# One GpSimd instruction per tap for both channel tiles of a prompt convolution, with the tap broadcast along the tokens

## The chip, the cores and the metric

The kernel runs on one core of a Trainium2 chip. The metric is device time in microseconds for one execution of the whole program, the median of the runs of one kernel. Instruction durations come from one profiled execution.

## The reference, cut to what matters

Two layers of a hybrid decoder trunk are computed for a prompt of 256 tokens and for 8 sample sequences of 4 tokens. Each layer is a feed-forward half step, a mixer, cross attention and another feed-forward half step. The mixer projects the normalised input once (`w_in`), and three groups use the columns: a gated depthwise convolution, a dilated attention, and an RWKV-7 recurrence. The convolution is this:

```python
glu = cols_a[..., :CONV_CH] * sigmoid(cols_a[..., CONV_CH:])
u = concatenate([hist, glu], axis=1)             # hist: 30 rows, zero for the prompt
y = conv_general_dilated(u, conv_w[:, None, :], window_strides=(1,), padding='VALID',
                         feature_group_count=CONV_CH) + conv_b
# then a layer norm over the 256 channels and silu
```

It has 256 channels and 31 taps, and it multiplies each channel by its own 31 weights.

## The kernel before

Activations lie with channels on the 128 partitions and the tokens along the row: 256 prompt tokens and then 32 sample tokens (T = 288, TP = 256). The 256 convolution channels are two channel tiles.

**Weights.** SP streams the weights in slabs. ScalarE (ACT) rounds each unit of 128x1024 to `w_hi` (line 1336), VectorE (DVE) computes the remainder `w_lo` = raw - `w_hi` (line 1837), and TensorE (PE) multiplies in three passes, hi*hi, lo*hi and hi*lo (lines 641 to 643). There are three such buffers (NW = 3), so that DVE can be at most three units ahead of PE. The order of work on each engine is written out by hand, and every engine is in order.

**The projection stage.** While PE computes the tiles of `w_in`, DVE does, between one `w_lo` and the next, the token shift of the tile that has arrived (`shifted`, lines 1932 and 1934), and pieces of the recurrence's preparation: the decay scan (1981), centring (1990), key norms (1995, 1997, 2002, 2006), products (2011 to 2030), and the 32 sample tokens' convolution (`conv_samples`, 1970 to 1975). Then the recurrence's chunk inverses follow (`block_products` on PE, line 827, with masks and sums on DVE, lines 2075 to 2113).

**The prompt convolution** runs on GpSimd (POOL) alone. `up` holds the 30 rows of history and 256 tokens of both channel tiles, `ycv` is the sum, and `prod` has two buffers of products, so that the products of tap k+1 are made before tap k is summed. For tap 0 the product and the bias go straight to `ycv`. For each other tap there are two `tensor_scalar` instructions (line 513), one for each channel tile, each with the 128 weights of that tap as a pointer to one value in each partition, and one `tensor_tensor` add over both tiles (line 529). POOL waits on its own semaphore before it overwrites `prod` and before it sums. It begins when the last gated tile is there (line 1949). Behind it on POOL's queue are the load of the cross-attention memory and the stores of the layer (lines 532 and 476). The sum of the last tap is waited for by ACT, before it overwrites the place of `prod`, and by PE, for the mean over channels (line 1052).

Of the kernel before, what the change touches and what calls it, by code (L numbers as in the profile page):

```python
# [9 lines left out]
ALU = mybir.AluOpType  # L10
# [3 lines left out]
P = 128  # L14
DEPTH, D_MODEL, D_FF = 2, 1024, 2816
TP, DEC_BATCH, DEC_SEQ = 256, 8, 4
# [7 lines left out]
TAPS = 31  # L24
# [80 lines left out]
PAR, NPAR = {}, 0  # L105
# [124 lines left out]
def program(nc, x_in, mem_in, stream, small, consts, conv_hist, wkv_in, copies, outs, known=None):  # L230
    (y_out, conv_out, kv_out, shift_out, wkv_p_out, wkv_s_out, memk_out, memv_out) = outs
    known = known or {}
    with ExitStack() as ctx:
# [45 lines left out]
        def take(*dims):  # L279
            n = int(np.prod(dims))  # L280
            v = arena[:, top[0]:top[0] + n]
            top[0] += n
            assert top[0] <= ARENA, top[0]
            if len(dims) == 1:
                return v
            names = "abcd"[:len(dims)]
            return v.rearrange(f"p ({' '.join(names)}) -> p {' '.join(names)}",
                               **{k: d for k, d in zip(names[1:], dims[1:])})
# [45 lines left out]
        up = take(2, HIST + TP)  # L334
# [34 lines left out]
        ycv, prod = take(2, T), take(2, 2, T)  # L369
# [50 lines left out]
        def bt(ap):  # L420
# [13 lines left out]
        TL, VL, SL, PL = (Line(s, known.get(n)) for s, n in ((tensor_done, "t"), (vector_done, "v"), (scalar_done, "s"),  # L434
                                                             (pool_done, "p")))
# [6 lines left out]
        @block.sync  # L442
        def _(sp):
            sp.dma_start(x[:], x_in).then_inc(start_landed, 16)

            first = CON["turn"]
            sp.dma_start(con[:, 0:first], consts[:, 0:first]).then_inc(start_landed, 16)
            gains = PAR["conv_w"]
            sp.dma_start(par_all[:, :, 0:gains], small[:, :, 0:gains]).then_inc(par_landed, 16)
            flat = stream.rearrange("l n p c -> (l n) p c")  # L450
            for l in range(DEPTH):
                for n in range(NSLAB):

                    held = n - NSLOT if n >= NSLOT else n + NSLOT * (ROUNDS - (n >= REST))
                    line, name = (VL, ("lo", UNIT_OF_SLAB[held] + 1)) if held in UNIT_OF_SLAB else (TL, ("slab", held))
                    if held == 0:
                        sp.wait_ge(vector_done, VL.value(l - 1, ("next", "lo", 1)))
                    else:
                        sp.wait_ge(line.sem, line.value(l, name) if n >= NSLOT else line.value_before(l, name))
                    sp.dma_start(slots[:, n % NSLOT, :], stream[l, n]).then_inc(slab_landed[n % NSLOT], 16)  # L460
                    if l == 0 and n == NSLOT + 4:
                        sp.dma_start(con[:, first:], consts[:, first:]).then_inc(con_landed, 16)
                        sp.dma_start(par_all[:, :, gains:], small[:, :, gains:]).then_inc(con_landed, 16)

                    if n % 5 == 4 and n // 5 < len(copies):
                        src, dst = copies[n // 5]
                        sp.dma_start(dst[l], src[l]).then_inc(copied, 16)
            sp.wait_ge(copied, 16 * 6 * DEPTH)


        @block.gpsimd
        def _(pool):
            n_stores = [0]

            def store(dst, src, name):
                pool.dma_start(dst, src).then_inc(stored, 16)
                n_stores[0] += 1
                stores[name] = n_stores[0]

            def presum(l, tag, n):  # L480

                for k in range(1, n):
                    pool.wait_ge(scalar_done, SL.value(l, (tag, "sq", k)))
                    if k > 1:
                        pool.wait_ge(pool_done, PL.value(l, (tag, "added", k - 1)))
                    PL.done(nc.gpsimd.tensor_tensor(sq[:, 0, :], sq[:, 0, :], sq[:, k, :], ALU.add), (tag, "added", k))  # L486

            pool.sem_inc(pool_done, PL.tail)
            PL.begin_prologue()
            presum(-1, "next", EARLY)  # L490
            pool.wait_ge(con_landed, 32)
            for l in range(DEPTH):
                n_stores[0] = 0
                PL.begin_layer()

                presum(l, "mix", EARLY)

                pool.wait_ge(vector_done, VL.value(l, ("ffn1", "x", KT - 1)))
                pool.wait_ge(tensor_done, TL.value(l, ("ffn1", "down", 1)))
                pool.dma_start(us4[:, :, :, 0:HIST], conv_hist[l]).then_inc(layer_landed, 16)  # L500


                pool.wait_ge(vector_done, VL.value(l, ("glu", 1)))
                pool.wait_ge(tensor_done, TL.value(l, ("in", "cols", RAW - 1)))
                par = par_all[:, l, :]

                def products(tap):
                    for ch in range(2):
                        w = par[:, PAR["conv_w"] + ch * TAPS + tap:PAR["conv_w"] + ch * TAPS + tap + 1]
                        bias = par[:, PAR["conv_b"] + ch:PAR["conv_b"] + ch + 1]  # L510
                        out = (prod[:, tap % 2, ch, :] if tap else ycv[:, ch, :])[:, 0:TP]
                        if tap:
                            p_ = nc.gpsimd.tensor_scalar(out, up[:, ch, tap:tap + TP], w, None, ALU.mult)  # L513
                        else:
                            p_ = nc.gpsimd.tensor_scalar(out, up[:, ch, tap:tap + TP], w, bias, ALU.mult, ALU.add)
                        PL.done(p_)
                    PL.done(p_, ("products", tap))

                products(0)
                products(1)  # L520
                for tap in range(1, TAPS):
                    if tap + 1 < TAPS:
                        if tap > 1:
                            pool.wait_ge(pool_done, PL.value(l, ("summed", tap - 1)))
                        products(tap + 1)
                    pool.wait_ge(pool_done, PL.value(l, ("products", tap)))
                    if tap > 1:
                        pool.wait_ge(pool_done, PL.value(l, ("summed", tap - 1)))
                    PL.done(nc.gpsimd.tensor_tensor(ycv[:, :, 0:TP], ycv[:, :, 0:TP], prod[:, tap % 2, :, 0:TP], ALU.add), ("summed", tap))  # L529

                pool.wait_ge(scalar_done, SL.value(l, ("u", 1)))
                pool.dma_start(memx, mem_in).then_inc(mem_landed, 16)
                store(conv_out[l, :, :, 0:HIST], up[:, :, TP:TP + HIST], "conv_p")
                store(conv_out[l, :, :, HIST:].rearrange("p a (b t) -> p a b t", b=DEC_BATCH)[:, 0],
                      us4[:, 0, :, DEC_SEQ:], "conv_s0")
                store(conv_out[l, :, :, HIST:].rearrange("p a (b t) -> p a b t", b=DEC_BATCH)[:, 1],
                      us4[:, 1, :, DEC_SEQ:], "conv_s1")
                pool.wait_ge(vector_done, VL.value(l, "shift_out"))
                store(shift_out[l], shift_o, "shift")

                pool.wait_ge(vector_done, VL.value(l, "roped"))
                pool.wait_ge(scalar_done, SL.value(l, ("in", IN_TILES - 1)))
                store(kv_out[l], qkv[:, G:3 * G, :], "kv")
                pool.wait_ge(vector_done, VL.value(l, ("state", 1)))
                store(wkv_p_out[l], st, "wkv_p")
                pool.wait_ge(vector_done, VL.value(l, "wkv_s"))
                store(wkv_s_out[l], wkv_s, "wkv_s")
                presum(l, "xattn", PRESUM["xattn"])
                pool.wait_ge(scalar_done, SL.value(l, ("kx", KT - 1)))
                store(memk_out[l], kx, "memk")  # L550
                pool.wait_ge(scalar_done, SL.value(l, ("vx", 7)))
                store(memv_out[l], vx, "memv")
                presum(l, "ffn2", PRESUM["ffn2"])
                PL.begin_tail()
                presum(l, "next", EARLY)
            assert n_stores[0] == NSTORE
            pool.wait_ge(vector_done, VL.value(DEPTH - 1, ("final", "h", KT - 1)))
            pool.dma_start(y_out, h[:]).then_inc(stored, 16)
            pool.wait_ge(stored, 16 * (NSTORE * DEPTH + 1))
# [1963 lines left out]
```

## Time and profile before

| what | value |
|---|---|
| median of 3 runs | 1712.31 us (1711.0 to 1713.2) |
| the profiled execution's own time | 1711.11 us |
| its span, first to last instruction | 1709.3 us |
| mean granted TensorE clock | 0.974 |
| busy shares of the span: PE, DVE, ACT, POOL | 94%, 63%, 44%, 17% |
| POOL's products (line 513), 120 instructions | 145.4 us |
| POOL's sums (line 529), 60 instructions | 87.7 us |

The shares are averages over all stages. The convolution runs twice, once in each layer, from 258.9 us to 379.3 us and from 1096.9 us to 1218.1 us of the span.

### The profile page before, as it was taken

How to read it: one execution, taken by the hardware profiler on the slowest of the kernel's cores; microseconds unless marked ns; L12 is line 12 of the kernel's file. 1: busy time of each engine (PE TensorE's matmuls, PEld its weight loads, DVE VectorE, ACT ScalarE, POOL GpSimd, SP SyncE). 2: the span in 40 equal slices, each digit the busy share in tenths (PEclk: the TensorE clock that was granted, in tenths of full speed). 3: DMA queues.
4: the chain of work that ended last, by engine and by line, in shares of the span. 5: the costliest groups of instructions: out<-in, count | busy, mean ns of one | idle time of the engine just before them, and what ended most of it. 6: DMA issues, size and time to landing. Idle time of an engine off the chain costs nothing.

```text
span 1709.3 us, 32132 instructions
## 1 busy us (share of the span) xinstructions
PE 1602.4 (94%) x13704; PEld 1512.7 (88%) x13704; DVE 1071.7 (63%) x1613; ACT 752.4 (44%) x1292; POOL 288.7 (17%) x250
## 2 busy tenths in 40 slices
PE   6999999899899889999999999998988997999996
PEld 6999998786789769999999999888768885999996
DVE  5776469867563357775577754896575642677744
ACT  5444357325453335443454434662254442544433
POOL 0000009990010010000000000399501000100000
PEclk9999999998999989999999999999889998999998
DMA  6666744204545764455355676431234468444450
GB/s 242 254 243 250 294 139 148 94 23 92 211 137 209 285 256 164 160 172 173 147 185 210 222 288 235 147 124 46 59 124 168 170 227 349 168 170 162 160 172 28
DMA packets 39247, 303.72 MB, mean 178 GB/s; under 512 B 4737, under 2 KB 4897, under 8 KB 6305
## 3 DMA queue, kind: packets, MB, share of 16 engines
q1 hardware_dynamic: 36624, 287.74, 46.5%
q0 software_dynamic: 2192, 12.35, 2.5%
q8 instruction: 109, 1.79, 0.4%
q10 hardware_dynamic: 288, 1.57, 0.3%
q14 instruction: 34, 0.27, 0.0%
HBM read 291.88 MB, written 36.83 MB: 192 GB/s over the span
## 4 chain that ended last, share of the span: by engine, by line
PE 79%; DVE 13%; ACT 4%; DMA 2%; issue 1%; SPq 0%; POOL 0%; DVEq 0%; ACTq 0%
PE bank L641 22%; PE bank L643 21%; PE bank L642 21%; DVE w_lo L1837 3%; PE bank L827 3%; DMA slots<-stream 2%; ACT w_hi L1336 1%; PE bank L1252 1%; PE bank L1288 1%; PE bank L1237 1%; DVE h_mem L1853 1%; PE bank L654 1%; ACT arena L1336 1%; PE bank L791 1%; PE bank L1125 1%
## 5 line engine op out<-in xcount | busy, mean ns | idle before, releaser
L1837 DVE TENSOR_TENSOR w_lo<-slots,w_hi 128x1024 fp32r<-128x1024 f32 x386 | 483.4, 1254 | 351.2 <-ACT w_hi L1336 350.6
L641 PE MATMUL bank<-h_hi,w_hi 128*128 128x288 f32 x1936 | 578.6, 299 | 30.1 <-DVE w_lo L1837 14.2
L642 PE MATMUL bank<-h_lo,w_hi 128*128 128x288 f32 x1936 | 572.4, 296 | 0.0
L643 PE MATMUL bank<-h_hi,w_lo 128*128 128x288 f32 x1936 | 570.4, 295 | 0.0
L1336 ACT CAST w_hi<-slots 128x1024 fp32r<-128x1024 f32 x390 | 406.9, 1045 | 296.9 <-PE bank L643 271.5
L641 PEld LDWEIGHTS bank<-h_hi,w_hi 128*128 128x128 f32 x1936 | 363.9, 188 | 37.9 <-issue 15.0
L643 PEld LDWEIGHTS bank<-h_hi,w_lo 128*128 128x128 f32 x1936 | 365.8, 189 | 0.0
L642 PEld LDWEIGHTS bank<-h_lo,w_hi 128*128 128x128 f32 x1936 | 364.7, 188 | 0.3
L486 POOL TENSOR_TENSOR arena<-arena 128x288 f32<-128x288 f32 x39 | 36.9, 945 | 1043.1 <-ACT arena L1376 618.0
L643 PE MATMUL bank<-hid_hi,w_lo 128*128 128x288 f32 x704 | 207.7, 295 | 0.0
L642 PE MATMUL bank<-hid_lo,w_hi 128*128 128x288 f32 x704 | 207.3, 294 | 0.0
L641 PE MATMUL bank<-hid_hi,w_hi 128*128 128x288 f32 x704 | 207.1, 294 | 0.0
L1336 ACT COPY arena<-bank 128x256 f32<-128x256 f32 (+8 forms) x258 | 86.0, 369 | 258.1 <-PE bank L643 117.1
L513 POOL TENSOR_SCALAR arena<-arena,par_all 128x256 f32<-128x256 f32 x120 | 145.4, 1222 | 5.5
L641 PEld LDWEIGHTS bank<-hid_hi,w_hi 128*128 128x128 f32 x704 | 132.1, 188 | 0.0
L643 PEld LDWEIGHTS bank<-hid_hi,w_lo 128*128 128x128 f32 x704 | 132.1, 188 | 0.0
L642 PEld LDWEIGHTS bank<-hid_lo,w_hi 128*128 128x128 f32 x704 | 132.0, 188 | 0.0
L1405 ACT ACTIVATE arena<-arena 128x288 f32<-128x288 f32 x88 | 39.2, 445 | 196.1 <-DVE arena L1868 196.1
L529 POOL TENSOR_TENSOR arena<-arena 128x512 f32<-128x512 f32 x60 | 87.7, 1461 | 0.3
L1868 DVE TENSOR_TENSOR arena<-bank,rs 128x288 f32<-128x288 f32 x88 | 40.3, 457 | 43.3 <-PE bank L643 43.0
L827 PE MATMUL bank<-arena 64*64 64x64 f32 x1488 | 54.0, 224 | 8.8 <-DVE arena L2098 7.2
L827 PEld LDWEIGHTS bank<-arena 64*64 64x64 f32 x1488 | 51.3, 139 | 11.3 <-DVE arena L2098 7.6
(323 smaller groups left out, 2130.8 us busy)
## 6 DMA issues: line engine op xcount, KB each, us to landing
slots<-stream SPq DMA_DIRECT2D x244, 1024.0 KB, 5.0
out_win3k<-win3k SPq DMA_DIRECT2D x2, 4080.0 KB
out_win3v<-win3v SPq DMA_DIRECT2D x2, 4080.0 KB
out_win2k<-win2k SPq DMA_DIRECT2D x2, 2032.0 KB
out_win2v<-win2v SPq DMA_DIRECT2D x2, 2032.0 KB
con<-consts SPq DMA_DIRECT2D x1, 2340.0 KB, 11.0
arena<-mem_in POOLq DMA_DIRECT2D x2, 1024.0 KB, 5.5
out_memk<-arena POOLq DMA_DIRECT2D x2, 1024.0 KB
```

The lines of the kernel that those rows point to most:

```text
L486: PL.done(nc.gpsimd.tensor_tensor(sq[:, 0, :], sq[:, 0, :], sq[:, k, :], ALU.add), (tag, "added", k))
L513: p_ = nc.gpsimd.tensor_scalar(out, up[:, ch, tap:tap + TP], w, None, ALU.mult)
L529: PL.done(nc.gpsimd.tensor_tensor(ycv[:, :, 0:TP], ycv[:, :, 0:TP], prod[:, tap % 2, :, 0:TP], ALU.add), ("summed", tap))
L641: mm(out, lhs[0], rhs[0], start=start, stop=False)
L642: mm(out, lhs[0], rhs[1], start=False, stop=False)
L643: return mm(out, lhs[1], rhs[0], start=False, stop=stop)
L654: i = mm(bank[7][:, 0:n], ones, squares[:, k, 0:n], start=k == 0, stop=k == KT - 1)
L827: i = mm(bank[b][o_, s_], lhs[r_, s_], rhs[r_, s_], start=True, stop=True)
L1336: return SL.done(nc.scalar.copy(out, in_), name)
L1405: SL.done(fn(th[:, t % 2, :], gs[:, t % 2, :], ACT.Tanh, scale=0.5), (tag, "tanh", t))
L1837: D(tt(out, src, hi.bitcast(F32), ALU.subtract), name)
L1868: D(tt(gs[:, t % 2, :], bank[gb][:, 0:T], rs[:], ALU.mult), (tag, "gated", t))
```

## The change

Tap 0 stays as it was. For taps 1 to 30 the two `tensor_scalar` products of 128x256 become one `tensor_tensor` product of 128x512, whose second input is the pair of weights of the tap, each broadcast along the 256 tokens. The sums, the two product buffers and the waits stay.

```diff
+                weights = par[:, PAR["conv_w"]:PAR["conv_w"] + 2 * TAPS].rearrange("p (c k) -> p c k", c=2)
+
                 def products(tap):
+                    if tap:
+                        w = weights[:, :, tap:tap + 1].to_broadcast([P, 2, TP])
+                        p_ = nc.gpsimd.tensor_tensor(prod[:, tap % 2, :, 0:TP], up[:, :, tap:tap + TP], w, ALU.mult)
+                        PL.done(p_, ("products", tap))
+                        return
                     for ch in range(2):
-                        w = par[:, PAR["conv_w"] + ch * TAPS + tap:PAR["conv_w"] + ch * TAPS + tap + 1]
                         bias = par[:, PAR["conv_b"] + ch:PAR["conv_b"] + ch + 1]
-                        out = (prod[:, tap % 2, ch, :] if tap else ycv[:, ch, :])[:, 0:TP]
-                        if tap:
-                            p_ = nc.gpsimd.tensor_scalar(out, up[:, ch, tap:tap + TP], w, None, ALU.mult)
-                        else:
-                            p_ = nc.gpsimd.tensor_scalar(out, up[:, ch, tap:tap + TP], w, bias, ALU.mult, ALU.add)
-                        PL.done(p_)
-                    PL.done(p_, ("products", tap))
+                        p_ = nc.gpsimd.tensor_scalar(ycv[:, ch, 0:TP], up[:, ch, 0:TP], weights[:, ch, 0:1], bias, ALU.mult, ALU.add)
+                        PL.done(p_, ("products", 0) if ch else None)
```

## Rows read from the trace of the kernel before

**Rows 1.** The page: busy shares, the chain that ended last, engines and lines.

```profile
PE 1602.4 (94%) x13704; PEld 1512.7 (88%) x13704; DVE 1071.7 (63%) x1613; ACT 752.4 (44%) x1292; POOL 288.7 (17%) x250
PE 79%; DVE 13%; ACT 4%; DMA 2%; issue 1%; SPq 0%; POOL 0%; DVEq 0%; ACTq 0%
```

**Rows 2.** Busy time by stretch: start:end, length, then each engine's us (instructions), clock.

```profile
258.00:322.00 64.00, 59.01 (x410) 55.39 (x408) 61.99 (x79) 37.63 (x75) 61.87 (x41) 0.97 0.38 132
322.00:380.00 58.00, 51.95 (x1056) 47.43 (x1056) 35.76 (x65) 18.98 (x39) 55.58 (x52) 1.00 0.11 34
1096.00:1160.00 64.00, 59.99 (x428) 56.79 (x427) 59.90 (x84) 37.56 (x75) 62.04 (x40) 1.00 0.41 138
```

**Rows 3.** Busy time of line 529 alone in the same stretches.

```profile
258.00:322.00 64.00, 19.57 (x12) 0.97 0.38 132
...
1096.00:1160.00 64.00, 19.75 (x12) 1.00 0.41 138
```

**Rows 4.** Instructions by line on POOL, whole span.

```profile
L513 POOL TENSOR_SCALAR arena<-arena,par_all 128x256 f32<-128x256 f32 x120 | 145.4, 1222 | 5.5
L529 POOL TENSOR_TENSOR arena<-arena 128x512 f32<-128x512 f32 x60 | 87.7, 1461 | 0.3
```

**Rows 5.** Lines 513 and 529: min/median/max in ns.

```profile
L513 POOL TENSOR_SCALAR arena<-arena,par_all x120: 917/925/3262, 261.2 to 1214.3; 128x256 f32<-128x256 f32 x120
...
L529 POOL TENSOR_TENSOR arena<-arena x60: 1267/1286/2516, 266.7 to 1216.8; 128x512 f32<-128x512 f32 x60
```

**Rows 6.** POOL and PE in order of time, first convolution's end and its reader.

```profile
376.58 2.72 POOL L529 TENSOR_TENSOR arena<-arena 128x512 f32<-128x512 f32 x2
...
402.82 1.81 PE L1052 MATMUL bank<-arena,con 128*128 128x288 f32 x3
```

**Rows 7.** DVE in order of time, projection stage of the first layer.

```profile
284.32 2.32 DVE L1837 TENSOR_TENSOR w_lo<-slots,w_hi 128x1024 fp32r<-128x1024 f32 x1
...
289.79 1.21 DVE L1837 TENSOR_TENSOR w_lo<-slots,w_hi 128x1024 fp32r<-128x1024 f32 x1
...
311.32 1.21 DVE L1837 TENSOR_TENSOR w_lo<-slots,w_hi 128x1024 fp32r<-128x1024 f32 x1
312.45 2.14 DVE L2015 SCALAR_TENSOR_TENSOR arena<-arena 128x864 f32<-128x864 f32 x1
314.51 1.05 DVE L2016 TENSOR_TENSOR arena<-arena 128x864 f32<-128x864 f32 x1
```

**Rows 8.** POOL in order of time, the same stage.

```profile
284.18 1.38 POOL L529 TENSOR_TENSOR arena<-arena 128x512 f32<-128x512 f32 x1
...
289.92 3.13 POOL L513 TENSOR_SCALAR arena<-arena,par_all 128x256 f32<-128x256 f32 x2
...
311.51 2.17 POOL L529 TENSOR_TENSOR arena<-arena 128x512 f32<-128x512 f32 x1
313.77 2.50 POOL L513 TENSOR_SCALAR arena<-arena,par_all 128x256 f32<-128x256 f32 x1
```

**Rows 9.** DVE by line, 258 to 322 us.

```profile
L1837 DVE TENSOR_TENSOR w_lo<-slots,w_hi 128x1024 fp32r<-128x1024 f32 x16 | 22.0, 1373 | 0.2 <-ACT w_hi L1336 0.2
L1932 DVE SCALAR_TENSOR_TENSOR arena<-arena,par_all 128x256 f32<-128x256 f32 x11 | 7.3, 661 | 1.3 <-ACT arena L1459 1.3
...
L1934 DVE SCALAR_TENSOR_TENSOR arena<-arena,par_all 128x32 f32<-128x32 f32 x11 | 4.7, 426 | 0.0
```

**Rows 10.** The same lines' shortest in the span (min/median/max).

```profile
L1932 DVE SCALAR_TENSOR_TENSOR arena<-arena,par_all x22: 380/526/1350, 260.5 to 1134.0; 128x256 f32<-128x256 f32 x22
...
L1934 DVE SCALAR_TENSOR_TENSOR arena<-arena,par_all x22: 237/377/1287, 260.9 to 1134.3; 128x32 f32<-128x32 f32 x22
```

**Rows 11.** DVE by line, 322 to 380 us, and its shortest in the span.

```profile
L2106 DVE TENSOR_TENSOR arena<-arena,con 128x384 f32<-128x384 f32 x8 | 7.5, 939 | 0.0
...
L2106 DVE TENSOR_TENSOR arena<-arena,con x16: 544/700/1679, 336.9 to 1191.7; 128x384 f32<-128x384 f32 x16
```

**Rows 12.** The chain that ended last, shares by line within 258 to 322 us.

```profile
by line: DVE w_lo L1837 23.5%; PE bank L641 7.1%; PE bank L750 6.8%; PE bank L643 6.7%; PE bank L642 6.6%; DVE arena L1932 4.5%; DVE arena L1970 4.0%; DVE arena L1934 3.5%; DVE arena L2022 3.2%; DVE arena L2015 3.2%; DVE arena L1997 3.0%; D
```

## The prediction

> **What bounds the kernel now.** I read the page first. PE is busy for 94% of the span and the chain that ended last runs 79% through PE, 13% through DVE and 0% through POOL [rows 1]. So POOL's own 233 us of convolution [rows 4] are nowhere a term of the time, and a faster POOL gains nothing by being faster. That has to be checked where POOL ends: the last sum of the first layer ends at 376.58 + 2.72 = 379.3 us, and PE reads the sum from 402.8 us [rows 6], with no wait for POOL. The convolution has 23 us to spare. What the change does to the time must therefore come through something that POOL shares with another engine.
>
> Second I read the busy time by stretch. In the projection stage, 258 to 322 us, DVE is busy 61.99 of 64 us, and PE 59.0; in the second layer it is 59.9 and 60.0 [rows 2]. In this stage the chain goes through DVE's lines more than through PE's: line 1837 alone has 23.5%, with 1932, 1970, 1934, 2022, 2015 and 1997 behind it [rows 12]. DVE waits there for hardly anything (0.2 us for ACT at line 1837, 1.3 us at line 1932 [rows 9]). So any microsecond that DVE loses in this stage is lost to the kernel, once in each layer, but for a small lead. The next stage, 322 to 380 us, has DVE busy for 35.8 of 58 us [rows 2]; there a DVE delay counts only when PE waits for that instruction.
>
> Third I laid DVE's and POOL's instructions side by side in time. The sum of line 529 starts at 284.18 and ends at 285.56. DVE's line 1837 starts at 284.32, takes 2.32 us in place of 1.21, and ends at 286.64 [rows 7, 8]: it lost 1.11 us, which is what was left of the sum. The other way round, the sum that starts at 311.51, during a line 1837 that ends at 312.53, takes 2.17 us, 0.90 more than its shortest of 1.267 [rows 5, 7, 8]. It got through exactly when DVE's instruction ended; the next one, line 2015, had started at 312.45 and took 2.14 where its neighbour of the same size, line 2016, took 1.05 [rows 7]. It waited until the sum was over. So a two-input POOL instruction and a DVE instruction that reads two SBUF tensors exclude each other for nearly their whole length, and at this boundary the waiting POOL instruction went ahead of the next DVE instruction.
>
> The products of line 513 behave otherwise. Two of them start at 289.92, while line 1837 runs from 289.79, and that one takes its 1.21 us as if alone. The product at 313.77 takes 2.50 us, and meanwhile line 2016 runs its 1.05 [rows 7, 8]. The single-input product is delayed by DVE but hardly delays DVE.
>
> The Trainium skill, page "SBUF — State Buffer", section "Who interferes with whom", says that the pair of ports that both engines use is an exclusive lock, and that a DVE instruction with two SBUF inputs and a GpSimd instruction that reads SBUF block each other fully. For the sums the trace agrees, with 1.11 us. For the products it doesn't: by that rule line 1837 at 289.79 should have been held up for part of 0.9 us. Which of the two holds for the products decides the sign of this change, and the rule's result is the first rival below.
>
> **The change part by part.**
>
> Removed: 30 pairs of products a layer, 2 x 0.917 = 1.83 us uncontended. Off the path, since POOL isn't on it: 0. What they cost DVE now is small; I come to it in the sum.
>
> Added: 30 `tensor_tensor` products of 128x512 a layer. The trace has no GpSimd product with a broadcast input. The nearest row is the sum of the same opcode and shape, 1.267 us at the shortest [rows 5]; I take it, because size, type and number of inputs are the same. The ends are one `tensor_scalar`, 0.917 us, and two of them, 1.83 us. The broadcast itself I take as free.
>
> What DVE loses now in the stage: 12 sums lie in it in each layer [rows 3]. At 1.11 us each these are 13.3 us; some met DVE in the middle of an instruction and cost less, and the products add a little: three lines alone lose 16 x (1.373 - 1.21) + 11 x (0.661 - 0.380) + 11 x (0.426 - 0.237) = 2.6 + 3.1 + 2.1 = 7.8 us [rows 9, 10], in 38 of the 79 instructions, so 15 us for all is a fair value. DVE's own work in the stage is then 62 - 15 = 47 us, in 79 instructions, 0.6 us each.
>
> What DVE loses after: POOL now has 60 two-input instructions a layer, with nothing between them in which DVE has the ports to itself (today the two products give it that room). If each takes its turn with one DVE instruction, a turn lasts 1.11 + 0.6 = 1.7 us, and 60 of them 103 us, all of it within the stage, since DVE has 79 instructions there. I let 5 of the 60 pass beside DVE instructions that read PSUM or have one input (a choice), and charge 55 x 1.11 = 61 us. The stage becomes 47 + 61 + 2 = 110 us in place of 64. That is 61 - 15 = 46 us more in each layer, 92 in all.
>
> What hides it: DVE's lead over PE. There are only three buffers, and PE waits 64 - 59 = 5 us already [rows 2]. I take off 3 us a layer (a choice; 0 is the other end). -6.
>
> What comes back: today 18 of the 30 sums fall in the next stage, where line 2106 loses 8 x (0.939 - 0.544) = 3.2 us [rows 11]. POOL will be done by the time DVE gets there. With the neighbouring masks I take 4 us a layer on the path. -8.
>
> POOL's end: 258.9 + 103 plus the two products of tap 0 and the passes is about 370 us of the span, near today's, while its readers move back by some 40. The stores and the memory load behind it on POOL's queue wait for later events of ACT and DVE and move with these. The semaphore increments that go away and those waits cost nothing, because POOL is in no chain. PE idles more in the stage, and its granted clock, 0.97 there [rows 2], may fall; PE needs 59 us and gets 110, so even slower matmuls are covered by DVE, and I charge 0.
>
> Sum: 92 - 6 - 8 = +78 us. Against the profiled execution's 1711.1 us this is 1789; the median, 1712.3, is 1.2 us above it, so 1790.
>
> **Rivals.**
>
> *The rule as the page has it: any POOL instruction holds up DVE.* Then today's products cost DVE as much as the sums, and POOL occupies the ports for 61.9 of 64 us [rows 2]. It still would, and the loss in the stage stays at 15 us; but with 30 instructions fewer POOL is done some 20 us sooner in the next stage, and gives back the 4 us there. Time: 1712 - 8 = 1704. For it: POOL is less busy in total. Against: the 1.21 and 1.05 us of lines 1837 and 2016 beside running products [rows 7, 8]. It decides if a single-input product now costs DVE 0.8 us or more. Chance 0.07. This is the case on the other side of zero. By the Trainium skill (same page and section), it would be the outcome.
>
> *The new product holds DVE as briefly as the old one,* because its second input is only two values a row. Then a tap takes POOL about 3.0 us in the stage, 20 sums fall in it instead of 12, 8 x 1.0 more, less 3 of lead and 3 in the next stage: +2 a layer, 1716. Against: the second input is still read as a tensor. Chance 0.10, half of it within the noise.
>
> *DVE wins every second boundary.* Two DVE instructions pass for each POOL instruction: 47/1.2 = 39 turns x 1.11 = 43 us, so the stage grows by 28, less 3 of lead and 2 in the next stage, +23 a layer: 1758. For it: the short DVE instructions (0.24 us, line 1934 [rows 10]) may slip in between two POOL ones. Chance 0.17.
>
> **How the numbers follow.** The forecast, that they take turns, has 0.63 and its own range is 1760 to 1830: below, a 0.917 us product (30 x 0.35 = 10 us less a layer, 1770) with a few more passes; above, all 60 at 1.25 us, no lead and nothing back, 2 x (75 - 15) = +120, 1832; a 1.83 us product alone gives 30 x 0.56 x 2 = +34, 1824. The third rival widens the range to 1740. The first two stay outside with 0.17, and 0.03 for what I haven't thought of. I take 1740 to 1830. 0.2%, 3.4 us, is about what a measurement of this kernel can tell from no change. Slower: 0.63 + 0.17 + 0.05 + 0.01 = 0.86. Same: 0.05 + 0.01. Faster: 0.07 + 0.01.
>
> **What the changed profile would show.** Products of 128x512 at about 1.27 us shortest and well over 1.5 mean. In the projection stage, DVE's line 1837 at 2.3 us in most places, 1932 near 1.5 and 1934 near 1.3, PE waiting for line 1837, and a stage of about 110 us instead of 64. In the next stage, line 2106 at 0.55. I am wrong if line 1837 stays near 1.3 us, if the new product's shortest is far from 1.27, or if DVE's losses don't show up in PE's waits.

## The result and the profile after

The changed kernel takes 1760.7 us (median of 4 runs, 1759.3 to 1763.1) against 1711.9 us for the kernel before beside it. The ratio is 1.0286, 95% interval 1.0268 to 1.0304: 49 us slower. The forecast was slower, 1790, range 1740 to 1830. So the sign was right, and the size was 78 where 49 was measured. The time is nearer to the third rival's 1758; why that is luck stands below.

Line numbers after the convolution's code are one higher than before. The page of the changed kernel:

```profile
PE 1623.0 (92%) x13704; PEld 1529.1 (87%) x13704; DVE 1125.2 (64%) x1613; ACT 754.1 (43%) x1292; POOL 245.4 (14%) x190
...
PE 76%; DVE 16%; ACT 3%; DMA 2%; issue 1%; SPq 0%; DVEq 0%; POOL 0%; ACTq 0%
...
L530 POOL TENSOR_TENSOR arena<-arena 128x512 f32<-128x512 f32 x60 | 107.0, 1783 | 0.3
L512 POOL TENSOR_TENSOR arena<-arena,par_all 128x512 f32<-128x512 f32 x60 | 83.0, 1385 | 4.4
```

POOL has 43 us less to do than in [rows 1], is still 0% of the chain, and the kernel is slower. The chain's share moved from PE to DVE. Both POOL lines together take 190 us against 233 before [rows 4], yet each sum now takes 1.78 us in the mean where it took 1.46. The busy time by stretch, columns as in [rows 2]:

```profile
258.00:350.00 92.00, 69.08 (x408) 63.99 (x407) 91.51 (x80) 38.20 (x75) 89.19 (x57) 0.85 0.26 91
350.00:380.00 30.00, 26.83 (x695) 25.38 (x696) 21.45 (x44) 9.38 (x19) 7.00 (x6) 1.00 0.20 65
1124.00:1216.00 92.00, 68.55 (x408) 63.66 (x407) 91.55 (x79) 37.90 (x74) 89.69 (x57) 0.85 0.26 90
```

The DVE instructions that filled 62 of 64 us now fill 91.5 of 92, in both layers, while PE waits. DVE by line in the first stretch, which answers to [rows 9]:

```profile
L1838 DVE TENSOR_TENSOR w_lo<-slots,w_hi 128x1024 fp32r<-128x1024 f32 x16 | 23.7, 1482 | 0.0
L1933 DVE SCALAR_TENSOR_TENSOR arena<-arena,par_all 128x256 f32<-128x256 f32 x11 | 12.9, 1170 | 0.0
L1935 DVE SCALAR_TENSOR_TENSOR arena<-arena,par_all 128x32 f32<-128x32 f32 x11 | 10.6, 961 | 0.0
L1971 DVE TENSOR_TENSOR arena<-arena,par_all 128x248 f32<-128x248 f32 x8 | 10.3, 1351 | 0.1
```

The two token-shift lines grew from 0.66 to 1.17 us and from 0.43 to 0.96 us in the mean, and the weight remainder in the first line only from 1.37 to 1.48. Why shows in DVE's and then POOL's instructions in order of time:

```profile
263.22 1.21 DVE L1838 TENSOR_TENSOR w_lo<-slots,w_hi 128x1024 fp32r<-128x1024 f32 x1
264.36 1.51 DVE L1933 SCALAR_TENSOR_TENSOR arena<-arena,par_all 128x256 f32<-128x256 f32 x1
265.80 1.02 DVE L1935 SCALAR_TENSOR_TENSOR arena<-arena,par_all 128x32 f32<-128x32 f32 x1
266.74 1.21 DVE L1838 TENSOR_TENSOR w_lo<-slots,w_hi 128x1024 fp32r<-128x1024 f32 x1
...
341.81 2.28 DVE L1838 TENSOR_TENSOR w_lo<-slots,w_hi 128x1024 fp32r<-128x1024 f32 x1
```

```profile
263.21 2.38 POOL L530 TENSOR_TENSOR arena<-arena 128x512 f32<-128x512 f32 x1
265.67 1.10 POOL L512 TENSOR_TENSOR arena<-arena,par_all 128x512 f32<-128x512 f32 x1
266.74 2.38 POOL L530 TENSOR_TENSOR arena<-arena 128x512 f32<-128x512 f32 x1
```

The sum at 263.21 waits while 1838 runs, then holds up 1933 until 265.6. The product at 265.67 holds up 1935 until about 266.6. 1935 is 32 elements long and over at once; 1838 and the next sum start in the same hundredth, 266.74, and 1838 goes first. So three DVE instructions pass for two of POOL here, not two for two. In the last 22 us of the stage DVE's other instructions are long too (128x864 most of them). There the turns are one for one, and line 1838 takes 2.06 to 2.30 us, as at 341.81; its other twelve take 1.21, or 1.45 once.

### The profile page after: what moved, and what is told of

It is laid out like the page before. It is cut to its first block, busy times and chain, and to the rows that moved or that the text cites. A ratio compares the mean times of both kernels' runs of the same rounds, so it can differ in the third digit from the quotient of the medians.

```text
span 1759.1 us, 32072 instructions
## 1 busy us (share of the span) xinstructions
PE 1623.0 (92%) x13704; PEld 1529.1 (87%) x13704; DVE 1125.2 (64%) x1613; ACT 754.1 (43%) x1292; POOL 245.4 (14%) x190
## 4 chain that ended last, share of the span: by engine, by line
PE 76%; DVE 16%; ACT 3%; DMA 2%; issue 1%; SPq 0%; DVEq 0%; POOL 0%; ACTq 0%
PE bank L642 21%; PE bank L644 21%; PE bank L643 20%; DVE w_lo L1838 4%; PE bank L828 3%; DMA slots<-stream 2%; DVE arena L1933 1%; DVE arena L1971 1%; DVE arena L1935 1%; ACT w_hi L1337 1%; PE bank L1253 1%; PE bank L1289 1%; PE bank L1238 1%; DVE h_mem L1854 1%; PE bank L655 1%
## 5 line engine op out<-in xcount | busy, mean ns | idle before, releaser
L642 PE MATMUL bank<-h_hi,w_hi 128*128 128x288 f32 x1936 | 588.7, 304 | 62.1 <-DVE w_lo L1838 43.8
L643 PE MATMUL bank<-h_lo,w_hi 128*128 128x288 f32 x1936 | 581.4, 300 | 0.0
L644 PE MATMUL bank<-h_hi,w_lo 128*128 128x288 f32 x1936 | 579.0, 299 | 0.0
L642 PEld LDWEIGHTS bank<-h_hi,w_hi 128*128 128x128 f32 x1936 | 372.8, 193 | 73.2 <-DVE w_lo L1838 22.3
L644 PEld LDWEIGHTS bank<-h_hi,w_lo 128*128 128x128 f32 x1936 | 374.3, 193 | 0.0
L643 PEld LDWEIGHTS bank<-h_lo,w_hi 128*128 128x128 f32 x1936 | 373.3, 193 | 0.3
L530 POOL TENSOR_TENSOR arena<-arena 128x512 f32<-128x512 f32 x60 | 107.0, 1783 | 0.3
L512 POOL TENSOR_TENSOR arena<-arena,par_all 128x512 f32<-128x512 f32 x60 | 83.0, 1385 | 4.4
L1869 DVE TENSOR_TENSOR arena<-bank,rs 128x288 f32<-128x288 f32 x88 | 40.2, 457 | 43.3 <-PE bank L644 43.1
```

The costliest lines, as they stand in the source:

```text
L512: p_ = nc.gpsimd.tensor_tensor(prod[:, tap % 2, :, 0:TP], up[:, :, tap:tap + TP], w, ALU.mult)
L642: mm(out, lhs[0], rhs[0], start=start, stop=False)
L643: mm(out, lhs[0], rhs[1], start=False, stop=False)
L644: return mm(out, lhs[1], rhs[0], start=False, stop=stop)
L1869: D(tt(gs[:, t % 2, :], bank[gb][:, 0:T], rs[:], ALU.mult), (tag, "gated", t))
```

## The experiments

Each comparison is with the kernel before on the same chip.

**Products alone and sums alone.** One kernel drops the sums, the other the products of taps 1 to 30.

```diff
# products alone (the loop's body, cut)
-                    PL.done(nc.gpsimd.tensor_tensor(ycv..., ycv..., prod[:, tap % 2, :, 0:TP], ALU.add), ("summed", tap))
+                    pool.wait_ge(pool_done, PL.value(l, ("products", tap - 1)))
+                    products(tap)
# sums alone (the same loop, cut)
-                        products(tap + 1)
...
+                    PL.done(nc.gpsimd.tensor_tensor(ycv..., ycv..., up[:, :, tap:tap + TP], ALU.add), ("summed", tap))
```

> The changed kernel without the 60 sums of line 530 (the convolution's result is then only tap 0 and the last products lie unused). My theory: each two-input GpSimd instruction costs VectorE about 0.8 us in the projection stage, product or sum alike; 30 products a layer cost 24 us where the kernel before lost 15, and the next stage is free of GpSimd (4 to 6 us back a layer), so 1712 + 2 x (9 - 5) = 1720, in 1705 to 1735. Rival, that the broadcast product holds VectorE only briefly and the crowding of the sums made the loss: about 0.15 us each, 2 x (4.5 - 15 - 5), but PE bounds the stage at 59 us, so no better than 1697 to 1702.

> The changed kernel without the products of taps 1 to 30 (the sums add the input itself, unweighted). If every two-input instruction costs the same 0.8 us: 1720 like the products alone. If a sum costs its full 1.1 us, because with a gap behind every sum VectorE still loses each boundary in front of one: 33 us a layer where 15 were, less 5, 1712 + 26 = 1738. The rival that only products hurt gives 1697 to 1702.

Measured: products alone 1726.0 us, ratio 1.0078 (1.0057 to 1.0098); sums alone 1728.9, 1.0102 (1.0086 to 1.0118). Busy time up to the end of the projection stage, products alone and then sums alone:

```profile
258.00:330.00 72.00, 61.17 (x393) 57.34 (x392) 70.24 (x82) 38.17 (x74) 45.74 (x32) 0.91 0.34 117
```

```profile
258.00:334.00 76.00, 61.41 (x396) 57.42 (x397) 74.14 (x87) 38.92 (x75) 50.36 (x32) 0.91 0.33 111
```

DVE's own work is 47 us, so 30 products cost it 23 us, 0.77 each, and 30 sums 27 us, 0.9 each. Either alone, with 32 POOL instructions a layer in the convolution where the kernel before had 92, is slower than the kernel before, by 0.8% and 1.0%. The rivals by which the new product is nearly harmless (1697 to 1702) fall. Products alone lay in the expected range, 1705 to 1735, and the sums between my two numbers, 1720 and 1738.

**The convolution begun later**, in the changed kernel and in the kernel before.

```diff
                 pool.wait_ge(tensor_done, TL.value(l, ("in", "cols", RAW - 1)))
+                pool.wait_ge(vector_done, VL.value(l, "shift_out"))
```

> The changed kernel with one more wait: GpSimd begins the convolution when VectorE has finished the projection stage (the shift output, after line 2062). Theory (the loss is VectorE held up in the stage that it bounds): the stage falls from 92 to about 60 us, the bound of TensorE; the next stage takes all 60 two-input instructions, 73 us uncontended and some 85 contended, loses 5 to 8 us there, and ends a few us after its reader would want it (some 84 us behind the start): about +5 a layer, 1722, in 1705 to 1740. Rival (the loss is TensorE's clock, 0.85 granted in the stage, or GpSimd's own instructions wherever they run): 1750 or more.

> The kernel before with the same later begin. Its convolution needs 30 x 3.16 = 95 us uncontended, so it ends some 15 us after its reader wants it: -4 in the stage, +15 to 20 behind, about 1712 + 2 x 14 = 1740. If it is no slower than the changed kernel begun as late, a faster convolution is worth nothing even there.

Measured: the changed kernel begun later takes 1710.9 us, ratio 1.0001 (0.9987 to 1.0016); all 49 us are gone. The kernel before begun as late takes 1740.5, 1.0168 (1.0153 to 1.0184), as expected. So the broadcast product is worth 30 us where the convolution begins so late that its end is waited for. The changed one's busy time by stretch:

```profile
258.00:314.00 56.00, 55.94 (x405) 53.34 (x405) 48.01 (x84) 37.50 (x74) 0.00 (x0) 1.00 0.44 151
314.00:372.00 58.00, 50.95 (x1042) 47.16 (x1040) 33.84 (x59) 18.46 (x38) 55.69 (x48) 0.94 0.10 34
```

Without POOL the stage is PE's, 55.9 of 56 us, at the full granted clock, and DVE has 48 us of work, which confirms the 47 of the sum. POOL's same instructions, run in the next stage, do less harm. They undo what is won in the stage (8 to 9 us in the first layer; it ends at 314 in place of 322): 5 to 6 us go before the two rope instructions (the rotation of queries and keys), and about 4 at them. POOL is busy until 391 us, and the rope instructions, whose medians are 0.45 and 0.46 us before, take 1.04 and 1.18:

```profile
L2130 DVE TENSOR_TENSOR arena<-arena,con x12: 490/1036/1042, 373.8 to 1225.1; 128x288 f32<-128x288 f32 x12
...
L2132 DVE TENSOR_TENSOR arena<-arena,h_mem x12: 1176/1180/1183, 374.3 to 1226.2; 128x288 f32<-128x288 f32 x12
```

In the kernel before, begun later, POOL ends at 415 us, and the reader that has to wait is ACT's, not PE's as I had written. Who waited for whom, 395 to 425 us:

```profile
PE bank L1022 <- ACT arena L1337: 22.6, 1, 22.6
ACT arena L1595 <- POOL arena L530: 22.1, 1, 22.1
```

**One product for each channel tile**, still broadcast.

```diff
-                        w = weights[:, :, tap:tap + 1].to_broadcast([P, 2, TP])
-                        p_ = nc.gpsimd.tensor_tensor(prod[:, tap % 2, :, 0:TP], up[:, :, tap:tap + TP], w, ALU.mult)
+                        for ch in range(2):
+                            w = weights[:, ch, tap:tap + 1].to_broadcast([P, TP])
+                            p_ = nc.gpsimd.tensor_tensor(prod[:, tap % 2, ch, 0:TP], up[:, ch, tap:tap + TP], w, ALU.mult)
+                            PL.done(p_)
```

> The changed kernel with its broadcast product split into two tensor_tensor products, one for each channel tile (128x256). If VectorE pays for the time that GpSimd's reads hold the ports, two short ones cost about what one long one does (2 x 0.45 us): 1755 to 1775. If it pays the same 0.78 us for each instruction that it meets, 90 of them instead of 60 cost 23 us more a layer: 1800 or more.

Measured: 1731.0 us, ratio 1.0114 (1.0096 to 1.0132). Both expectations were wrong: more instructions, and 30 us less than the changed kernel. Busy time, and DVE's short shift line:

```profile
258.00:332.00 74.00, 61.51 (x412) 57.56 (x411) 73.55 (x81) 37.53 (x74) 72.27 (x57) 0.95 0.33 113
```

```profile
L1937 DVE SCALAR_TENSOR_TENSOR arena<-arena,par_all 128x32 f32<-128x32 f32 x11 | 6.7, 605 | 0.0
```

In the stage DVE loses 73.6 - 47 = 27 us to 57 POOL instructions, 0.47 each. The changed kernel's 57 cost 91.5 - 47 = 44.5 us, 0.78 each. Each DVE instruction can be laid beside the same one in the changed kernel begun later, where POOL is silent in this stage. What it takes longer is the hold that the POOL instruction beside it had on DVE. By this, a product of 128x256 that holds DVE costs it 0.38 us, one of 128x512 0.79, and a sum 1.03 to 1.04 in both kernels. So DVE pays by the length of what it meets, as the first theory had it. But POOL has three instructions a tap here, and at each one it waits for DVE too: the stage holds some 18 taps, where the changed kernel's holds 28 and the kernel before's 12 or 13. The loss for each tap is 15/12.5 = 1.2 us before, 1.5 with two short products, 1.6 in the changed kernel; by these figures, how many taps go through while DVE is the bound matters more than what each costs. I worked this out from the windows of the three kernels; it fits them, and no run varied the number of broadcast taps alone. For the old products, the six-tap and ten-tap versions further down do: DVE's loss in the first layer's stage is 6.4 and 11.2 us, 1.2 for each tap more.

**A full tensor as the product's second input**, so the result is another one.

```diff
-                        w = weights[:, :, tap:tap + 1].to_broadcast([P, 2, TP])
+                        w = up[:, :, 0:TP]
```

> The changed kernel with a full tensor (the first 256 tokens of the input, both tiles) as the product's second input in place of the broadcast weights; the result is another one. It tells where the product's 1.04 us come from. If the broadcast is what makes the product 0.2 us shorter than the sum: shortest 1.26 us here, 30 x 0.2 = 6 us more a layer, about 1772. If multiplying is shorter than adding, or the output being another tensor than the inputs: shortest stays 1.04 and the time 1761.

Measured: 1765.7 us, ratio 1.0317 (1.0297 to 1.0337). The product's shortest, median and longest:

```profile
L512 POOL TENSOR_TENSOR arena<-arena x60: 1040/1342/2621, 261.1 to 1221.9; 128x512 f32<-128x512 f32 x60
```

The shortest is 1.040 us, as with the broadcast (1.042), so the broadcast isn't what makes the product shorter than the sum. But the median is 1.342 where the changed kernel's is 1.106. The first six products take the same time in both kernels; of the later ones many take 1.3 us and more where the broadcast ones take 1.1. DVE loses 47.8 and 48.7 us in the two stages in place of 44.6 and 44.5. That covers the 5 us over the changed kernel. Why only the later products are longer is open.

**A wait at both boundaries.** Each product stands directly in front of its own sum.

```diff
-                products(1)
...
-                    if tap + 1 < TAPS:
...
-                        products(tap + 1)
...
+                    products(tap)
                     pool.wait_ge(pool_done, PL.value(l, ("products", tap)))
```

> The changed kernel with each product directly in front of its own sum and a wait between them, so that GpSimd has its gap of 0.09 us at both boundaries and not only behind a sum. Theory of the turns: VectorE's short instructions (0.24 us) now slip through at both boundaries and the loss for each GpSimd instruction falls from 0.78 to 0.6 us: some 10 us less a layer, 1740 to 1750. Rival (turns are strict whatever the gap): 1761 or a little more.

Measured: 1760.9 us, ratio 1.0287 (1.0272 to 1.0303), the changed kernel's time; the rival holds. The 0.09 us gap moved, and with it which POOL instruction waits for line 1834 (1837 in the kernel before), but the number that passes hardly did: 53 two-input ones in the stage in place of 55, and DVE loses 43.1 us in place of 44.6:

```profile
265.52 1.36 POOL L526 TENSOR_TENSOR arena<-arena 128x512 f32<-128x512 f32 x1
266.96 2.00 POOL L512 TENSOR_TENSOR arena<-arena,par_all 128x512 f32<-128x512 f32 x1
```

```profile
265.65 1.28 DVE L1931 SCALAR_TENSOR_TENSOR arena<-arena,par_all 128x32 f32<-128x32 f32 x1
266.85 1.21 DVE L1834 TENSOR_TENSOR w_lo<-slots,w_hi 128x1024 fp32r<-128x1024 f32 x1
```

**The short shift first.**

```diff
-                    D(stt(xs[:, t, 0:TP], f_p[:, t, 0:TP], pr("shift", t), xs[:, t, 0:TP], ALU.mult, ALU.add))
                     own = bt(xs[:, t, TP:T])
-                    D(stt(own, ..., own, ALU.mult, ALU.add), ("xs", t))
+                    D(stt(own, ..., own, ALU.mult, ALU.add))
+                    D(stt(xs[:, t, 0:TP], f_p[:, t, 0:TP], pr("shift", t), xs[:, t, 0:TP], ALU.mult, ALU.add), ("xs", t))
```

> The changed kernel with VectorE's two token-shift instructions in the other order: the short one (32 elements) first, the long one (256) right in front of line 1838. In the changed kernel the short one stood in front of 1838 and 1838 ran its 1.21 us undisturbed in most places (mean 1.48), while the long one had a mean of 1.17 and the short one of 0.96. Theory (whatever stands behind a held instruction that is short gets through, since VectorE asks again before GpSimd does): now 1838 is held, its mean rises to 2.0 or more, the long shift falls to 0.6 or less, and since a held instruction costs about the same whichever it is, the time stays near 1761 (1750 to 1770). Rival (1838 got through because it is long, or by the place of the sums in time): its mean stays near 1.5.

Measured: 1773.0 us, ratio 1.0354 (1.0337 to 1.0371). DVE by line, 258 to 356 us:

```profile
L1838 DVE TENSOR_TENSOR w_lo<-slots,w_hi 128x1024 fp32r<-128x1024 f32 x16 | 31.1, 1946 | 0.0
L1934 DVE SCALAR_TENSOR_TENSOR arena<-arena,par_all 128x32 f32<-128x32 f32 x11 | 11.2, 1017 | 0.0
...
L1935 DVE SCALAR_TENSOR_TENSOR arena<-arena,par_all 128x256 f32<-128x256 f32 x11 | 9.4, 856 | 0.0
```

The instruction behind the short one, now the long shift, loses less (1.17 to 0.86), and 1838, now behind the long one, is held up (1.48 to 1.95). That is the theory's direction, short of its 0.6 and 2.0. The time rose by 12 us, where I had allowed 9. One more thing follows: of the two orders, the one that lets the longest DVE instruction through is better for the kernel, since POOL waits longest behind it. With the short shift first, all 60 two-input POOL instructions fall in the stage in place of 55, and DVE loses 49.8 us in place of 44.6.

**A pause instead of a late begin.** Taps 0 to 6 with the old products and five sums at the start, then the wait for DVE's stage, then the other taps with the broadcast products.

```diff
+                    if tap and tap <= EARLY_TAPS:          # 6
+                        for ch in range(2):
+                            p_ = nc.gpsimd.tensor_scalar(prod[:, tap % 2, ch, 0:TP], up[:, ch, tap:tap + TP], weights[:, ch, tap:tap + 1], None, ALU.mult)
+                            PL.done(p_, ("products", tap) if ch else None)
+                        return
...
                 for tap in range(1, TAPS):
+                    if tap == EARLY_TAPS:
+                        pool.wait_ge(vector_done, VL.value(l, "shift_out"))
```

> A version meant to beat both: taps 0 to 6 as in the kernel before (single-input products, five sums) at the start, then a wait until VectorE has finished the projection stage, then the rest with the broadcast products. Without GpSimd the stage takes 56 us and is TensorE's (begun later, above), while VectorE has 49 us of work, so five sums at 1.1 us and the products are hidden; the remaining 24 taps take 24 x 2.5 = 60 us and end at about 375 us of the span, before the rope instructions that the late version held up. 1712 - 2 x 7 = 1698, in 1692 to 1706. Rival (the lead of three buffers is too small to hide even five sums, or the next stage loses what is won): 1708 to 1715.

Measured: 1700.7 us, ratio 0.9936 (0.9920 to 0.9952): 0.6% faster than the kernel before, a small gain but clear of 1, and near the expected 1698. Busy time by stretch:

```profile
258.00:314.00 56.00, 55.78 (x403) 53.09 (x402) 53.77 (x84) 37.05 (x74) 26.22 (x19) 1.00 0.43 149
314.00:372.00 58.00, 52.41 (x1050) 48.19 (x1050) 32.38 (x58) 18.94 (x39) 55.98 (x47) 0.97 0.10 34
```

The stage stays PE's (55.8 of 56) with DVE's 54 us hidden, and POOL ends at 375.7 us. Three kernels vary this one: ten taps early (`EARLY_TAPS` 10), broadcast products in the early taps too, and the kernel before with nothing but the pause:

```diff
# kernel before
                 for tap in range(1, TAPS):
+                    if tap == 6:
+                        pool.wait_ge(vector_done, VL.value(l, "shift_out"))
```

> The version with six taps early, with ten: nine sums and ten old products at the start (they run to about 302 us of the span), the other 20 taps with the broadcast product after the projection stage. VectorE has 7 us of room in the stage; nine sums cost it 10, so the stage grows by some 3 us a layer, and the convolution ends 10 us sooner than with six, where nobody waits for it: 1701 + 2 x (3 - 1) = 1705, in 1698 to 1709. Rival (the room is larger, and the next stage still suffered): 1697.

> The version with six taps early, but with the broadcast products there too. Five sums and six products at 0.78 us each are 8.6 us, at 1.1 and 0.85 us each 10.6 us, against 7 us of room: 2 to 4 us more a layer, 1704 to 1709. If a broadcast product in that stage were harmless: 1701 as with the old ones.

> The kernel before with the same pause: tap 0 to 6 at the start, the other taps after the projection stage, all products old. It tells what the broadcast product itself is worth where VectorE isn't the bound. 24 taps x 3.16 = 76 us and some contention end at 392 to 396 us of the span in place of 376: the rope instructions are held up and the reader, which wants the sum at about 396, is just served. 1706 to 1714. If it equals the six-taps version with the new products (1701), the change is worth nothing anywhere.

Measured: ten taps 1706.7 us, 0.9977 (0.9966 to 0.9989); new products early 1705.4, 0.9968 (0.9957 to 0.9979); old products throughout 1701.5, 0.9943 (0.9931 to 0.9956). The first two came as expected: with nine sums the stage of the first layer grows from 55 to 60 us, so the room is used up. Six broadcast products in that stage in place of twelve old ones cost DVE 4 us more in each layer (10.3 in place of 6.4), the stage grows by 2, and the kernel is 4 to 5 us longer. The third did not come as expected. The pause alone gives the whole gain, and the broadcast product adds nothing to it that can be measured. Its POOL ends 19 us later, and ACT just has to wait for it, 1.96 us; POOL and ACT in order of time:

```profile
391.83 2.73 POOL L531 TENSOR_TENSOR arena<-arena 128x512 f32<-128x512 f32 x2
```

```profile
394.60 1.62 ACT L1596 ACTIVATE arena<-arena,con 32x384 f32<-32x384 f32 x3 [1.96 <-POOL arena L531]
```

Against those 2 us stand the old products' shorter holds between the projection stage and the ropes. One mask line there (by line, 320 to 420 us), first in the six-tap version with broadcast products and then in this one:

```profile
L2108 DVE TENSOR_TENSOR arena<-arena,con 128x384 f32<-128x384 f32 x2 | 3.0, 1504 | 0.0
```

```profile
L2101 DVE TENSOR_TENSOR arena<-arena,con 128x384 f32<-128x384 f32 x2 | 2.2, 1087 | 0.0
```

Both win 8.4 us in the first layer's stage. Up to the instruction of line 2075 that starts at 373 us in the kernel before, the version with broadcast products has lost 2.8 of them, this one 1.0. At the ropes this kernel, with POOL busy beside them, has medians of 0.80 and 0.54 us, where the changed kernel begun later had 1.04 and 1.18.

## Why the prediction was right in sign and too large

**POOL isn't on the path**: right. 43 us less POOL work, 49 us more time.

**Two-input POOL instructions and DVE exclude each other**: right. It is shown by products alone, by sums alone, and by the late begin, which removes the loss with the same instructions. The Trainium skill, page "SBUF — State Buffer", section "Who interferes with whom", states this lock, and for the two-input instructions these runs agree. Applied to the single-input products it would have made the change harmless. There the measurement decides: of the 27 old products in the first layer's stage none held a DVE instruction for more than 0.22 us, and the change wasn't harmless. The first rival is out.

The prediction's own evidence for this was weaker than it reads. Line 1837 at 289.79 had started 0.13 us before the product at 289.92, so it was the product that would have had to wait, lock or no lock; the two products took 3.13 us there, and not 1.83.

The prediction let DVE's one-input instructions pass. Some of them are held up all the same. The centring (`tensor_scalar`, with one tensor as input), by line, 258 to 350 us, first in the changed kernel and then in the same kernel begun later:

```profile
L1991 DVE TENSOR_SCALAR arena<-arena 128x128 f32<-128x128 f32 x6 | 4.8, 866 | 0.0
```

```profile
L1992 DVE TENSOR_SCALAR arena<-arena 128x128 f32<-128x128 f32 x6 | 1.3, 284 | 0.0
```

The reciprocal of the key norms (1.95 us) and the two `tensor_reduce` of the samples' convolution (1.19 each) take the same time in both, though POOL's two-input instructions run beside them.

**Each takes its turn, 55 x 1.11 = 61 us a layer**: this is the term that was mis-sized. DVE lost 44.6 us in the first layer's stage and 44.5 in the second's. DVE executes the same instructions in the same order in both kernels, so each can be laid beside itself in the changed kernel begun later, as above:

| first layer's stage | predicted | measured |
|---|---|---|
| two-input POOL instructions in it | 60 | 55 |
| of these, with next to no hold on DVE | 5 | 6 |
| holds by products | 1.11 us each | 26, 0.79 us each |
| holds by sums | 1.11 us each | 23, 1.03 us each |
| in all, with 0.4 us for tap 0 | 61 us | 44.6 us |

The shorter product makes 26 x 0.32 = 8 us of the difference of 16 to 17: it is 1.04 us at the shortest, and not 1.267. Six holds fewer make another 7, and the sums' 0.08 us the last 2. That DVE gets three instructions through for two of POOL makes no hold shorter. It slows POOL down, so that 5 of the 60 fall behind the stage; in the other order of the token shift all 60 fall in it, and DVE loses 49.8 us.

The third rival came near the time by luck. It had 39 holds of 1.11 us, 43 us in all, and there were 49, of 0.9 us in the mean.

**What DVE lost before, 15 us a layer**: the same comparison gives 15.1 us in the first layer and 12.2 in the second.

**The stage**, from DVE's last gated instruction (line 1949, now 1950) to its line 2058 (now 2059), took 91.4 us in place of 63.5 in the first layer, and 91.3 in place of 60.6 in the second. It grew by 59 us in all, where 92 were predicted.

**What comes back, -8, and the lead, -6**: the stages' 59 us less the profiled executions' 50 leave 9 us that came back. They came unevenly, though. In the second layer 8 us are gained between the stage and the layer's end. In the first layer 5 us are gained up to the end of the ropes and lost again behind them, for a reason that wasn't followed up. Nothing is left for the lead.

**POOL's end at about 370 us**: it was 357.3, 13 sooner, for which the shorter product is one reason. Nothing depended on it. The reader's deadline I had put at PE's 402.8 us; ACT's comes first: the kernel before begun later missed it by 22.1 us, and its six-tap version by 1.96.

**TensorE's clock, charged at 0**: the run bears it out. The mean granted clock of the stage fell from 0.97 to 0.85, so that a part of it ran at the lower of the clock's two levels, and PE was busy for 69 us instead of 59. DVE was busy for 91.5 of the 92 us, so PE's longer work was covered.

**The signs of being wrong.** Two of those that I had named came. Line 1838 has a mean of 1.48 us and takes 2.3 only at the end of the stage, and the product's shortest is 1.04 us. Both belong to the mis-sized term. The third did not come: PE waits for line 1838 for 16.8 us in this stage. Line 2107, 2106 before, has its 0.55 us in the next stage.

## What to carry to other kernels

Before reducing the number or the length of GpSimd instructions that aren't on the path, look at which of the new ones have two SBUF inputs, and at what VectorE does at that moment. Where VectorE is the bound, more two-input work pushed through costs VectorE about 0.8 us for each instruction here, however much GpSimd itself saves; look for a stage in which VectorE has room, and move or pause the work instead. A pause of one line gave 0.6% here, and the merged instruction nothing on top of it. Only where the convolution's end was waited for, in the versions begun later, was the merged instruction worth something (30 us).

## What the runs showed that I hadn't expected

The product of 128x512 takes 1.04 us at the shortest, with a broadcast or a full second input, and the sum of the same shape 1.26. The sum writes over one of its inputs and adds, the product writes elsewhere and multiplies; which of these makes the 0.22 us wasn't separated.

With two short two-input products for each long one the kernel takes 1731 us, and not 1761. The two together hold VectorE about as long as the one (2 x 0.38 against 0.79 us), so what fits the runs is that GpSimd, which waits at every boundary, gets less done in the stage: 18 taps and not 28.
